# Gate/up projections of four SwiGLU blocks as seven block products of half size, and down projections in 16 jobs between them

## The reference, cut to what matters

```
D_MODEL, SEQ, DEC_BATCH, D_FF = 1024, 512, 8, 2816

def _swiglu(x, w_gu, w_down):
    a, b = jnp.split(x @ w_gu, 2, axis=-1)
    return (jax.nn.silu(a) * b) @ w_down

def _trunk(x, ...):
    for i in range(2):
        x = x + 0.5 * _swiglu(_rmsnorm(x, norm_g[i, 0]), ffn_gu[i, 0], ffn_down[i, 0])
        hn = _rmsnorm(x, norm_g[i, 1])
        x = x + (_retention(hn, ...) if i % 2 == 0 else _gated_delta(hn, ...))
        x = x + 0.5 * _swiglu(_rmsnorm(x, norm_g[i, 2]), ffn_gu[i, 1], ffn_down[i, 1])
    return _rmsnorm(x, final_g), ...
```

## Time and profile before

| what | value |
|---|---|
| device time, median of 3 runs (lowest, highest) | 2615.48 us (2615.23, 2615.69) |
| profiled execution, span from the first to the last instruction | 2619.2 us |
| busy: PE, DVE, ACT, POOL | 2572.6, 1264.2, 821.0, 300.5 us |
| weights and states read, results written | 218.81 MB, 26.05 MB |
| stretch of the first block's slots after its first, by matmul count | 3072 matmuls in 369.24 us |

### The profile page before, as it was taken

One profiled execution on the slowest core, in us unless ns is written; L12 is line 12 of the kernel. 1 busy time (PEld: TensorE's weight loads), 2 busy tenths in 40 slices (PEclk: granted clock), 3 DMA queues, 4 the chain that ended last, 5 costly groups with the idle time before them and its releaser, 6 DMA issues.

```text
span 2619.2 us, 48630 instructions
## 1 busy us (share of the span) xinstructions
PE 2572.6 (98%) x20575; PEld 2484.8 (95%) x20575; DVE 1264.2 (48%) x1584; ACT 821.0 (31%) x1042; POOL 300.5 (11%) x307
## 2 busy tenths in 40 slices
PE   8999999999999999999999999999999998999998
PEld 8999999898989899999999999989998998999998
DVE  5444334646464654443244443377557755444422
ACT  4222222424242432222232222244433344222222
POOL 1000010202020210000000000002530353000000
PEclk9999999999999999999999999999999999999999
DMA  4332334524242333332343323321122111323232
GB/s 131 96 96 76 88 93 141 185 86 177 93 173 97 137 91 87 96 86 78 97 111 91 96 82 89 104 84 52 49 66 87 36 49 53 97 84 93 78 91 74
DMA packets 340333, 246.73 MB, mean 94 GB/s; under 512 B 9428, under 2 KB 320908, under 8 KB 340208
## 3 DMA queue, kind: packets, MB, share of 16 engines
q1 hardware_dynamic: 325856, 197.32, 25.6%
q0 software_dynamic: 14352, 47.58, 5.0%
HBM read 218.81 MB, written 26.05 MB: 93 GB/s over the span
## 4 chain that ended last, share of the span: by engine, by line
PE 95%; DVE 3%; ACT 1%; issue 0%; DMA 0%; SPq 0%; ACTq 0%; DVEq 0%
PE ps L743 61%; PE ps L934 17%; PE ps L1118 5%; PE ps L828 1%; PE ps L851 1%; PE ps L837 1%; PE ps L1062 1%; PE ps L1128 1%; PE ps L783 1%; PE ps L1099 1%; DVE wl L1672 1%; PE ps L1075 1%; PE ps L993 0%; DVE xl L1678 0%; DVE cv L2012 0%
## 5 line engine op out<-in xcount | busy, mean ns | idle before, releaser
L743 PE MATMUL ps<-xh,wh 128*128 128x260 f32 x2816 | 569.0, 283 | 3.7 <-DVE gate L2258 1.5
L743 PE MATMUL ps<-xh,wl 128*128 128x260 f32 x2816 | 568.3, 284 | 0.0
L743 PE MATMUL ps<-xl,wh 128*128 128x260 f32 x2816 | 567.5, 283 | 0.0
L1672 DVE TENSOR_TENSOR wl<-raw,wh 128x2048 fp32r<-128x2048 f32 (+1 forms) x204 | 428.7, 2102 | 266.7 <-ACT wh L1333 266.5
L1333 ACT ACTIVATE wh<-raw 128x2048 fp32r<-128x2048 f32 (+1 forms) x204 | 354.5, 1738 | 343.2 <-PE ps L743 189.2
L743 PEld LDWEIGHTS ps<-xh,wh 128*128 128x128 f32 x2816 | 435.4, 189 | 5.8 <-issue 2.7
L743 PEld LDWEIGHTS ps<-xh,wl 128*128 128x128 f32 x2816 | 435.1, 189 | 0.0
L743 PEld LDWEIGHTS ps<-xl,wh 128*128 128x128 f32 x2816 | 433.8, 189 | 0.0
L743 PE MATMUL ps<-hh,wh 128*128 128x260 f32 x1408 | 284.4, 283 | 0.0
L743 PE MATMUL ps<-hh,wl 128*128 128x260 f32 x1408 | 283.1, 282 | 0.0
L743 PE MATMUL ps<-hl,wh 128*128 128x260 f32 x1408 | 282.8, 282 | 0.0
(11 more groups left out here) (372 smaller groups left out, 2857.8 us busy)
## 6 DMA issues: line engine op xcount, KB each, us to landing
raw<-in_ffn_gu_dram SPq DMA_DIRECT2D x176, 512.0 KB, 4.9
raw<-in_ffn_down_dram SPq DMA_DIRECT2D x64, 384.0 KB, 3.5
raw<-in_ret_w_in_dram SPq DMA_DIRECT2D x48, 512.0 KB, 4.4
raw<-in_ffn_down_dram SPq DMA_DIRECT2D x64, 320.0 KB, 3.9
s_ring<-in_state_ret_dram POOLq DMA_DIRECT2D x32, 512.0 KB, 6.2
out_dram<-s_ring POOLq DMA_DIRECT2D x32, 512.0 KB, 3.4
raw<-in_gdn_w_in_dram SPq DMA_DIRECT2D x32, 512.0 KB, 4.5
raw<-in_ret_w_out_dram SPq DMA_DIRECT2D x16, 512.0 KB, 3.8
```

The lines of the kernel that those rows point to most:

```text
L743: m_ = nc.tensor.matmul(ps[:, 2 * q + h, 0:HALF], w_, v[:, kt0 + t, h * HALF:(h + 1) * HALF], start=b_, stop=e_)
L1672: nc.vector.tensor_tensor(wl[:, s, 0:cols], raw[:, s, 0:cols], wh[:, s, 0:cols].bitcast(F32), ALU.subtract).then_inc(w_low, 1)
```

## The change

Gate and up of one slot form a 2x2 block matrix: rows gate (1) and up (2), columns the even (1) and odd (2) tiles of the 1024 features. The activations form a 2x2 block matrix too: rows the even and odd tiles, columns the two halves of 260 tokens. In place of the eight block products of the ordinary rule, seven are made (numbered 1 to 7), from sums of blocks:

- of the weights: S1 = A21 + A22, S2 = S1 - A11, S3 = A11 - A21, S4 = A12 - S2. GpSimd makes the four for each slot, 128x512 each, in `raw` and `mixed` (`block_sum`)
- of the activations: four differences for each pair of tiles, made once in each SwiGLU block by VectorE (`x_mixed`). `xch` and `xcl` hold the seven splits
- of the results: products 1, 6, 7 and 4 accumulate in one bank, 5 and 3 in another, 2 in a third. ScalarE copies the state of the bank after 1, after 6 and (of the other) after 5 into `kept` (m1, u2, m5), and VectorE adds: C11 = 2 + m1, C12 = (5 + 3) + u2, C22 = (1 + 6 + 7) + m5. The block C21 is the bank itself after product 4

Each product is 4 tiles x 3 = 12 matmuls of 260 columns. A slot becomes a "G" job of 84 matmuls in the order 1, 2, 6, 5, 7, 3, 4. Splits are made by blocks in five groups ("A", "1", "2", "L", "4"; 7 blocks of 512 columns in place of 4) for the next job, into six single buffers and one double one. The down projection is cut into "D" jobs of two tiles of `x` and two or three pairs of rows of h (48 or 72 matmuls). 16 of them in each block are put between the G jobs, so `hh` and `hl` shrink to a ring of 12 tiles, and every D job adds to two tiles of `x`. All the jobs are written out where the slots of before were loops.

The core of the diff (parts of it are left out at "..."; the additions to `plan`, to buffers and to semaphore names are among these):

```diff
+def ffn_jobs():
+    G = lambda a_, b_: [("G", q, (0, 1, 2, 3)) for q in range(a_, b_)]
+    D_ = lambda m, pairs_: [("D", m, pairs_)]
+    out = G(0, 5)
+    for q, pairs_, more in ((5, (0, 1), 3), (11, (2, 3, 4), 3)):
+        for m in range(4):
+            out += D_(m, pairs_) + G(q + m, q + m + 1) if m < 3 else D_(m, pairs_)
+        out += G(q + 3, q + 3 + more)
+    out += D_(0, (5, 6, 7)) + G(17, 18) + D_(1, (5, 6, 7)) + G(18, 19) + D_(2, (5, 6, 7)) + G(19, 22) + D_(3, (5, 6, 7))
+    for m in range(4):
+        out += D_(m, (8, 9, 10))
+    return out
...
+PRODUCT_BLOCK = {1: 0, 2: 1, 5: 2, 6: 3, 3: 4, 7: 5}
+PRODUCT_GROUP = {1: "A", 2: "A", 5: "1", 6: "2", 3: "4", 7: "L", 4: "L"}
...
@@ GpSimd @@
+            def ffn(f):
+                for j in range(NJ + 1):
...
+                    if nxt and is_gate(nxt[1]):
+                        block_sum(*nxt, "2")
+                        block_sum(*nxt, "4")
...
+                    if nxt2 and is_gate(nxt2[1]):
+                        block_sum(*nxt2, "1")
+                        block_sum(*nxt2, "3")
...
@@ TensorE @@
+                def product(c, m, steps=range(KP)):
...
+                        if m in (1, 2, 5):
+                            bank_free(c, m)
+                        elif m == 4:
+                            v(f"C22.{c}")
+                        else:
+                            act_({6: "m1", 7: "u2", 3: "m5"}[m] + f".{c}")
+                        pe.wait_ge(blk_low, blocks_split(f, c, PRODUCT_GROUP[m]))
+                    o = ps[:, bank_of(c, m), 0:HALF]
+                    for t in steps:
...
+                        for n, (w_, r_) in enumerate(((hi_w, high), (hi_w, low), (lo_w, high))):
+                            m_ = nc.tensor.matmul(o, w_, r_, start=m in (1, 2, 5) and t == 0 and n == 0, ...)
...
@@ ScalarE, a G job @@
+                    if is_gate(j):
+                        if gate_before:
+                            silu(p)
+                        copy(j, "m1", 1, 0)
+                        if gate_before:
+                            h_high(p)
...
+                        high("A")
+                        copy(j, "u2", 6, 1)
+                        high("x")
+                        copy(j, "m5", 5, 3)
+                        high("12Lyz4")
...
@@ VectorE, a G job @@
+                    if is_gate(j):
...
+                        if gate_before:
...
+                            silu_scaled(p)
+                            second(p)
+                            first(p)
+                        upper(j)
+                        if gate_before:
+                            h_low(p)
...
+                        low("A1x")
+                        lower_sum(j)
+                        low("2y")
+                        upper_second(j)
+                        gate_scaled(j)
+                        low("L4z")
```

At the start of a SwiGLU block, VectorE's work for each tile n of `x` is:

```diff
+            def before_ffn(f, n):
+                m = n // 2
+                if n % 2:
+                    x_mixed(f, m, 0)
+                    if m:
+                        x_split(f, m - 1, True)
+                elif m:
+                    x_split(f, m - 1, False)
+                    for i in range(1, 4):
+                        x_mixed(f, m - 1, i)
+                if 4 <= n < 7:
+                    block_split(f, 0, "A12"[n - 4])
+                if n == KT - 1:
+                    x_split(f, m, False)
+                    for i in range(1, 4):
+                        x_mixed(f, m, i)
+                    block_split(f, 0, "4")
+                    x_split(f, m, True)
+                    block_split(f, 0, "L")
```

More of the change, by code:

```diff
@@ L39 @@
 SLOT = 16 * P
+TURNED_BANK = (0, 4, 5, 1, 2, 3, 1, 2)
 RH, RK, RV = 4, 256, 512
@@ new lines, in ffn_v_names @@
+def ffn_v_names():
+    out = []
+    for j in range(NJ + 1):
+        p, gate_before = j - 1, is_gate(j - 1)
+        if is_gate(j):
+            if j and not gate_before:
+                out += [f"XA.{p}", f"XB.{p}"]
+            if gate_before:
+                out += [f"sr.{p}", f"hB.{p}", f"hA.{p}"]
+            out.append(f"C11.{j}")
+            if gate_before:
+                out.append(f"hl.{p}")
+            out += [f"C12.{j}", f"C22.{j}", f"gr.{j}"] if j == 0 else [f"C22.{j}", f"C12.{j}", f"gr.{j}"]
+        elif gate_before:
+            out += [f"sr.{p}", f"hB.{p}", f"hA.{p}", f"hl.{p}"]
+        else:
+            out += [f"XA.{p}", f"XB.{p}"]
+    return " ".join(out)
@@ L85, with ffn_a_names @@
+def ffn_a_names():
+    out = []
+    for j in range(NJ):
+        before = is_gate(j - 1)
+        if before:
+            out.append(f"silu.{j - 1}")
+        if is_gate(j):
+            out.append(f"m1.{j}")
+        if before:
+            out.append(f"hh.{j - 1}")
+        if is_gate(j):
+            out += [f"m5.{j}", f"u2.{j}"] if j == 0 else [f"u2.{j}", f"m5.{j}"]
+    return " ".join(out)
+FFN_T = Steps(ffn_t_names())
+FFN_V = Steps(ffn_v_names())
+FFN_A = Steps(ffn_a_names())
 GH, GG, GC, LV = 8, 4, 4, 6
@@ L525, in _ @@
+            ffn(0)
+            ret_body(phases[0], 0)
+            with sp.Fori(1, RH) as h:
+                ret_body(phases[0], h)
+            ffn(1)
+            ffn(2)
+            for g in range(2):
+                gdn_body(phases[1], g)
+            ffn(3)
             for c, (done, n) in enumerate(((y_by_v, 1), (y_by_a, 1), (y_by_v, 2), (y_by_v, 3))):
```

1062 lines of the change are left out of this document (695 added, 367 removed).

## The result

The changed kernel is slower: **2685.9 us** in the median of 4 runs (2681.4 to 2691.8) against 2615.6 for the kernel before beside it, ratio 1.027, 95% interval 1.0254 to 1.0285. The forecast was 2557 us, and faster. The profiled execution's span is 2683.0 us (2619.2 before).

What follows compares the result with a forecast made beforehand. TensorE was taken to set the time: 2619.2 - 126.9 (matmuls) + 14.4 + 20 + 6.6 (job steps) + 24.1 (starts) + 2.9 (mixers, tail) = 2560.3, less 3.7 for the median: 2557 us. Likeliest 2530 to 2585; 8 in 10: 2506 to 2605.

Steps and rivals of the forecast that it cites:

- 126.9 us of matmuls removed: Gate/up slots of the four blocks: 1056 matmuls fewer at 0.1202 us each save 126.9 us.
- I take 0.15 each, 6.6 us: G jobs next to D jobs, 11 a block: 0.15 us lost each, 6.6 us together (0 to 20).
- Starts, 24.1 us: Starts of the four blocks: VectorE's added differences and splits, partly held by GpSimd's sums, cost 24.1 us (10 to 40).
- Steps from G to G, 34.4 us: G jobs behind G jobs: product 7 waits for u2; 14.4 us in runs of three, 20 in runs of five.
- The warning in the last sentence of the prediction: ScalarE's queue: waits laid out as hidden, above all the A split standing before u2, would make the forecast wrong; no size.
- Mixers' starts and tail, 2.9 us: Mixers' starts and kernel's tail: two late tiles where it was one, 0.7, 0.7 and 1.5, together 2.9 us.
- 41.0 were forecast: Jobs inside the four blocks: terms of 14.4 and 20 us for G behind G, 6.6 for G next to D.
- Rival D: Every GpSimd sum holds VectorE, which sets the pace: 40 G steps at 3.3 us more, 2648 us, slower; chance 0.11.

Runs made afterwards that it cites:

- experiment 5: Changed kernel with 16 useless matmuls more behind product 1 of every G job following a D job of two pairs: 2675.3 us against 2685.9.
- experiment 7: Changed kernel with ScalarE's copies m1 and m5 of each block's first job put before the late split of x and L split: 2681.4 us (1.0271).
- experiment 2: Changed kernel with ScalarE's copy u2 put before its split of A: 2714.0 us (1.0384), against 2685.9.
- experiment 4: Changed kernel with GpSimd's four sums a job replaced by eight memsets each, same waits, wrong weights: 2614.1 us (0.9999), against 2685.9.
- experiment 15: Changed kernel, queues reordered: additions to x, A items, first copies earlier; low part of h later; VectorE's PSUM-input work beside GpSimd's sums in G and D jobs: 2580.5 us (0.9877).
- experiment 9: Changed kernel with additions to x, A items and first copies earlier (2618.0 us), plus VectorE's hA and C11 beside GpSimd's sum 2, hB after: 2642.5 us.

## Why the prediction was wrong, point by point

- **126.9 us of matmuls removed: right as a price, and 5.8 of it counted twice.** 0.1202 us a matmul holds wherever the chain is unbroken. But the terms for the starts are differences up to job 1's first matmul, and the first job's 12 matmuls fewer lie before that: 4 x 1.44 = 5.8 us were taken off in both. Without this slip the same working gives 2563 us.
- **"I take 0.15 each, 6.6 us" for G jobs next to D jobs: the step that failed.** The prediction laid out 2 low of such a job and not the additions to x. They free the banks of the D job, product 2 needs one, and before them in VectorE's queue stands L low, which needs ScalarE's L split, which waits for the D job's last matmul. The waits are 49.5 us before these G jobs and 4.7 before D jobs. Moving that one item took 30 us of waits away and gained 46 with the clock.
- **No term for the clock: missed.** Up to 51 us in the blocks against 4 before; experiment 5 shows that the stands behind D jobs cause it in their places.
- **Starts, 24.1 us: mis-sized**, 66.5. This miss is as large as that behind the D jobs. The forecast let half of GpSimd's sums hold VectorE for 0.9. The differences took 971 ns in the mean rather than 430, the blocks' 128x512 low parts 866 to 914 ns, and most of the miss lies behind the last addition, where 13.4 us were laid out and 20.6 to 21.0 measured. Part of that is a low clock in the first job. ScalarE's copies stood behind its late split, but experiment 7 shows that this hid VectorE's lateness and little else.
- **Steps from G to G, 34.4 us: right in place, mechanism and size** (product 7 for u2, behind the high part of h and A in ScalarE's queue): 27.5 us of waits. Single steps differ. The holds in the ring were 2.1 us and not 1.0 to 1.6, so two steps of the first run stand 1.7 to 1.8, while the others of that run stand 1.0 or less. Behind four of the seven stands of 1.7 to 1.8 us the clock fell. The warning in the last sentence of the prediction pointed at A before u2; experiment 2 shows that swapping them makes it worse.
- **Mixers' starts and tail, 2.9 us: about right.** From the end of one block's matmuls to the first addition of the next, retention is 8.0 us shorter and the gated DeltaNet 1.2 longer; the tail is 2.0 longer. In retention the kernel before had a granted clock of 0.97 and the changed one 0.99, about 10 us of its 511, which is no merit of the change.
- **Sum:** 66.5 (starts) + 5.8 (counted twice) - 4.8 (mixers and tail) leave 190.7 - 67.5 = 123.2 us for the jobs inside the four blocks from job 1 on, where 41.0 were forecast. Of these 81.7 are the waits above (49.5 + 4.7 + 27.5). The granted clock there is 0.97, 0.98, 0.98 and 0.98, some 30 us. The rest isn't placed; most of it is what some 50 stands cost if the last matmul before each takes its whole 0.28 us and not 0.12 (an estimate).
- **Rival D named the right side and the wrong reason.** Its 2648 us came from 3.3 us in each of 40 steps. The sums cost 72 us in all, 72 / 88 = 0.8 a G job, and holds of 4.6 us in each of 88 jobs would have been 405. The Trainium skill's rule on the shared reads ("SBUF — State Buffer", section "Who interferes with whom") is borne out by VectorE's times in experiment 4 (914 against 701 ns), but far from every sum met an operation that it could hold. What made the change slower was both together: the order (68 us) and the sums (72), each of which alone would have left it level (2614 and 2618 us).
- In experiment 15's order the same matmuls and sums take 2580.5 us, 23 above the forecast. The forecast was made for the order as it was given, so this doesn't bear it out.

Still open is how the 51 us of clock divide between stands and other causes, why a stand of 2.35 us is followed by a low clock in some places and not in others, why the mixers' clock differs between executions, and how the sums' 72 us divide between VectorE's holds and GpSimd's own time. A version without sums at the blocks' starts alone wasn't tried, so the 66.5 us there aren't divided by experiment either.

## What to carry to other kernels

When fewer matmuls are bought with more work on the other engines, lay out every queue over every kind of junction (here G to G, D to G, G to D, the start), and for each product ask what frees its bank, not only what feeds it. Follow a late item around its ring before moving it: the operation that TensorE waits for by name may be the last link, and moving it can lengthen the ring (experiments 2 and 9). Where GpSimd reads SBUF beside VectorE, put VectorE's operations with a PSUM input beside it, and count one of the others that meets it at up to 1.8 us in place of 0.7. When an operation is left out to learn its price, check that what stands in for it lasts as long: otherwise two causes are taken away at once.

## What the runs showed of the hardware

- Of the changed kernel's twelve stands of 2.35 us behind D jobs six were followed by a granted clock of 0.50 (1.2 GHz) for about 3 us, of the four of 3.53 to 4.35 us all, and of the seven of 1.7 to 1.8 us between G jobs four, in three of the blocks the second of two in a row. The 72 matmuls behind one of 2.35 us took 10.25 us rather than 8.65, so the stand cost 1.6 us more than its length. Work of no use in the stand kept the clock at 1.00. Two of the stands of 2.35 us in block 1, the first followed by a clock of 1.00, the second by one of 0.63 over 4 us (busy us of TensorE and its matmuls, clock, DMA share, GB/s):

```profile
1038.00:1042.00 4.00, 3.55 (x30) 1.00 0.41 117
1057.00:1061.00 4.00, 4.00 (x23) 0.63 0.58 169
```

- GpSimd's memsets to SBUF leave VectorE's times alone (701 and 693 ns), GpSimd's sums do not (914 and 866 ns). Eight memsets of 128x64 take 0.76 us, one sum of 128x512 1.30 to 1.83 in the mean of its kind.
- The clock in the mixers, whose code is the same in all these kernels, was 0.97 to 1.00 in their windows, which is worth up to 15 us. Differences of that size between single traces say nothing of an edit.
